# A silu gate whose 1/(1+exp(-z)) is made on ScalarE as exp(-ln(1+exp(-z))), with VectorE clamping the input

## What is computed

```
y_att = o_att * jax.nn.silu(ag.astype(f32))
y_hg  = o_hg * jax.nn.silu(hg.astype(f32))
ret_out  = rms_norm(ro).reshape(B, S, RET_W) * jax.nn.silu(rg)
diff_out = (...) * jax.nn.silu(dg)
lru_out  = rg_lru(...) * jax.nn.silu(lg)
```

## Time and profile before

| | |
|---|---|
| median of 3 runs | 3411.26 us (3410.83 to 3414.91) |
| the profiled execution's own time | 3415.89 us |
| its span, first to last instruction | 3414.0 us |
| TensorE matmul busy | 3176.8 us, 93% |
| VectorE busy | 1807.2 us, 53% |
| ScalarE busy | 1129.8 us, 33% |
| GpSimd busy | 1307.2 us, 38% |
| mean granted TensorE clock | 0.968 |

### The profile page before, as it was taken

How to read it: one execution, slowest core, us unless ns; L and a number is a source line. 1 busy time by engine, 2 the same in 40 slices (tenths; PEclk the granted TensorE clock), 3 DMA queues, 4 the chain that set the end, 5 groups by cost and what they waited for, 6 DMA issues and landing times.

```text
span 3414.0 us, 43651 instructions
## 1 busy us (share of the span) xinstructions
PE 3176.8 (93%) x14102; PEld 2497.3 (73%) x14102; DVE 1807.2 (53%) x2314; ACT 1129.8 (33%) x2000; POOL 1307.2 (38%) x1005
## 2 busy tenths in 40 slices
PE   8999999999999997988999999989779999999895
PEld 6877777777777785866877777768667777777684
DVE  5867667544544315557365764451273756555413
ACT  5333333233333433333232223333332332333332
POOL 4433333333333343433433433334334434333344
PEclk9999999999999998988999999999899999999998
DMA  5322121122121421223322222132233222222322
GB/s 217 111 86 74 61 74 62 62 74 72 63 74 69 165 90 60 96 88 109 132 74 84 79 74 80 66 124 98 77 120 121 77 81 90 74 74 74 123 93 92
DMA packets 60424, 308.54 MB, mean 90 GB/s; under 512 B 5536, under 2 KB 5920, under 8 KB 28832
## 3 DMA queue, kind: packets, MB, share of 16 engines
q1 hardware_dynamic: 34992, 254.82, 21.0%
q10 hardware_dynamic: 25328, 52.37, 4.3%
HBM read 288.81 MB, written 18.35 MB: 90 GB/s over the span
## 4 chain that ended last, share of the span: by engine, by line
PE 65%; DVE 21%; DVEq 5%; issue 5%; ACT 2%; POOL 1%; ACTq 0%; DMA 0%; POOLq 0%
PE z L252 54%; DVE work L916 5%; PE scores L291 2%; DVE work L1046 2%; PE scores L375 1%; DVEq L1120 1%; PE o_bank L344 1%; DVE work L1035 1%; POOL w_low L215 1%; DVE work L910 1%; DVE work L974 1%; DVEq L1201 1%; DVE work L1182 1%; PE scores L325 1%; PE o_bank L310 1%
## 5 line engine op out<-in xcount | busy, mean ns | idle before, releaser
L215 POOL TENSOR_TENSOR w_low<-w_raw,w_high 128x512 fp32r<-128x512 f32 x968 | 1289.6, 1338 | 2077.9 <-ACT w_high L508 2067.2
L252 PE MATMUL z<-u_high,w_high 128*128 128x512 f32 x3744 | 1537.9, 411 | 87.8 <-DVE u_low L1167 38.3
L252 PE MATMUL z<-u_low,w_high 128*128 128x512 f32 x3744 | 1476.5, 394 | 0.0
L252 PE MATMUL z<-u_high,w_low 128*128 128x512 f32 x3744 | 1476.5, 394 | 0.0
L508 ACT ACTIVATE w_high<-w_raw 128x512 fp32r<-128x512 f32 x968 | 601.6, 628 | 1492.6 <-PE z L252 1454.5
L252 PEld LDWEIGHTS z<-u_high,w_high 128*128 128x128 f32 x3744 | 713.1, 190 | 300.4 <-issue 62.6
L252 PEld LDWEIGHTS z<-u_low,w_high 128*128 128x128 f32 x3744 | 714.2, 191 | 153.8 <-issue 13.4
L252 PEld LDWEIGHTS z<-u_high,w_low 128*128 128x128 f32 x3744 | 712.8, 190 | 154.8
L1182 DVE TENSOR_TENSOR work<-work 128x512 f32<-128x512 f32 x90 | 104.4, 1161 | 441.0 <-ACT work L688 427.1
L916 DVE RECIPROCAL work<-work 128x512 f32<-128x512 f32 x88 | 295.1, 3353 | 6.5
L910 DVE TENSOR_TENSOR work<-z,work 128x512 f32<-128x512 f32 x114 | 78.9, 692 | 182.8 <-PE z L252 173.0
(11 more groups left out here) (189 smaller groups left out, 2327.0 us busy)
## 6 DMA issues: line engine op xcount, KB each, us to landing
w_raw<-in_wt SPq DMA_DIRECT2D x243, 1024.0 KB, 4.7
out_hT<-work ACTq DMA_DIRECT2D x10, 1024.0 KB, 9.8
work<-in_xT ACTq DMA_DIRECT2D x8, 1024.0 KB, 12.5
work<-out_hT ACTq DMA_DIRECT2D x8, 1024.0 KB, 13.1
e_scratch<-work ACTq DMA_DIRECT2D x1, 4096.0 KB, 16.6
work<-e_scratch ACTq DMA_DIRECT2D x1, 4096.0 KB, 22.4
work<-in_gw ACTq DMA_DIRECT2D x2, 1792.0 KB, 11.8
work<-in_dec ACTq DMA_DIRECT2D x12, 256.0 KB, 2.6
```

The lines of the kernel that those rows point to most:

```text
L215: pool.tensor_tensor(WL[:, 4 * q:4 * q + 4, :], RAW[:, t.odd, 512 * q:512 * q + 512].rearrange("p (k c) -> p k c", k=4), WH[:, 4 * q:4 * q ...
L252: mm = pe.matmul(bank[:], w[:, k, :], u[:, k, :], start=(k == 0 and n == 0), stop=(k == KT - 1 and n == 2))
```

## The change

ScalarE's `gate_exp` at the 48 gates becomes `gate_sigmoid`: it waits for a new signal `g_bounded`, and makes exp(-x), ln(x + 1) and exp(-x) in place on TM, with a drain between each two. VectorE's new `bounded` writes TM = max(RW, -42) right behind `rstd_mul`, and signals. VectorE's `sigmoid_of` (add 1, reciprocal) goes from the gates. ScalarE no longer waits for `z_free` there. The other users of `sigmoid_of` and of `gate_exp` (the recurrence steps) stay as they were.

```diff
+GATE_MIN = -42.0
...
+            def gate_sigmoid(n):
+
+                act.wait_ge(sem("g_bounded"), n + 1)
+                act.activation(row(TM), row(TM), ACT.Exp, scale=-1.0)
+                act.drain()
+                act.activation(row(TM), row(TM), ACT.Ln, bias=ONES[:, 0:1])
+                act.drain()
+                act.activation(row(TM), row(TM), ACT.Exp, scale=-1.0).then_inc(sem("gexp"), 1)
+
...
-                    if (gate and p == 15) or (gates and q == 3):
-                        gate_exp(t.plus(s))
+                    if gate is not None and p == 15:
+                        gate_sigmoid(gate)
+                    if gates is not None and q == 3:
+                        gate_sigmoid(gates + s)
...
             def gate_exps(*tiles):
                 for m in tiles:
-                    gate_exp(Tile(T_HGG + m))
+                    gate_sigmoid(m)
...
                     for q in range(4):
                         high(t, q)
-                    gate_exp(t)
+                    gate_sigmoid(l * 16 + 26 + m)
...
+            def bounded():
+
+                v.drain()
+                v.tensor_scalar(row(TM), row(RW), GATE_MIN, None, ALU.max).then_inc(sem("g_bounded"), 1)
+
             def gate_tile(t, n, dst, bank=None):

                 rstd_mul(t, row(RW), bank)
+                bounded()
                 v.wait_ge(sem("gexp"), n + 1)
-                sigmoid_of(TM)
                 v.tensor_tensor(dst, row(RW), row(TM), ALU.mult)
                 v.drain()

...
                 rstd_mul(Tile(T_L2 + R_LG + 5, (PER_LAYER, l)), row(RW))
+                bounded()
                 low(l * 32 + 64, MIX[:], b=8)
                 v.drain()
                 v.wait_ge(sem("gexp"), gl + 16)
-                sigmoid_of(TM)
                 v.tensor_tensor(row(RW), row(RW), row(TM), ALU.mult)
```

More of the change, by code:

```diff
@@ L637, in _, with step @@
             WORK = {"hg": hg_work, "att": att_work, "ret": ret_work, "dif": dif_work}
-            def step(t, gate=False, gates=False, hg=False, work=None, j=None, between={}, **kw):
+            def step(t, gate=None, gates=None, hg=False, work=None, j=None, between={}, **kw):
                 for p in range(16):
@@ L785, in _ @@
                 step(Tile(T_HG, (4, i)), hg=True, work="hg", j=i - 1)
-            step(Tile(T_ATT), gate=True, work="hg", j=HG_HEADS - 1)
+            step(Tile(T_ATT), gate=8, work="hg", j=HG_HEADS - 1)
             act.wait_ge(sem("hg_done"), PRIMED + HG_HEADS)
             with act.Fori(1, PAIRS) as i:
-                step(Tile(T_ATT, (4, i)), gate=True, work="att", j=i - 1)
+                step(Tile(T_ATT, (4, i)), gate=i + 8, work="att", j=i - 1)
             def finished_tile(p):
@@ L866, in _ @@
                 act.dma_start(W[:, GW:GW + 7, :], gw[l].rearrange("p (r t) -> p r t", r=7)).then_inc(sem("gw_loaded"), 16)
[L867 removed]
+                step(Tile(T_L2 + R_RET, (PER_LAYER, l)), gate=l * 16 + 16)
                 for h in range(1, RET_HEADS + 1):
[L869 removed]
+                    step(Tile(T_L2 + R_RET + 4 * h, (PER_LAYER, l)), gate=l * 16 + (16 + h), work="ret", j=l * RET_HEADS + h - 1,
                          load=h if h < RET_HEADS else None, b=h - 1, cl=l + 1 if h == 1 else None)
@@ L873, in _ @@
                 with act.Fori(1, DIF_HEADS) as i:
-                    step(Tile(T_L2 + R_DIF, (PER_LAYER, l), (4, i)), gate=True, work="dif",
+                    step(Tile(T_L2 + R_DIF, (PER_LAYER, l), (4, i)), gate=l * 16 + i + 22, work="dif",
                          j=l * DIF_HEADS + i - 1)
-                step(Tile(T_L2 + R_LG, (PER_LAYER, l)), gates=True, work="dif", j=l * DIF_HEADS + DIF_HEADS - 1)
+                step(Tile(T_L2 + R_LG, (PER_LAYER, l)), gates=l * 16 + 26, work="dif", j=l * DIF_HEADS + DIF_HEADS - 1)
                 for m in range(4, LRU_TILES):
```

2 lines of the change are left out of this document (removed).

## The result

| | before | after |
|---|---|---|
| median of 4 runs each | 3412.01 us (3410.83 to 3414.91) | 3369.70 us (3366.53 to 3373.27) |
| the profiled execution's own time, its span | 3415.89, 3414.0 us | 3372.59, 3370.7 us |
| TensorE matmul busy | 3176.8 us, 93% | 3167.0 us, 94% |
| VectorE, ScalarE busy | 1807.2, 1129.8 us | 1650.3, 1191.4 us |
| mean granted TensorE clock | 0.968 | 0.971 |

The ratio is 0.9873, with a 95% interval of 0.986 to 0.9887: 42 us faster, 43.3 between the two profiles. The forecast was 3362 us, a gain of 49.

A forecast was written before the change was run, and what follows sets the result against it. TensorE, nearly full, was taken to bound the kernel, so only its idle time behind gates counts: waits 38.4 us plus clock 11.2 make 49.6, say 49, giving 3362 us; range 3345 to 3389.

The forecast's parts named there:

- The gate's own price: Each changed gate, norm product to gate product: 2.7 us instead of 4.76, so 2.0 us shorter on VectorE.
- a maximum that runs at half pace: Pessimistic bound on one gate: slower maximum and 0.3 us more per drain make it 3.7 us, saving only 1.0.
- First gates and attention: Ahead of the layers: TensorE's wait at 108.05 goes, 1.4 us; 2.0 us of attention's single 6.6 us wait comes back.
- Retention: Retention steps: TensorE's ten 0.5 us waits for the decay product go, 5.2 us in all.
- Differential: Differential steps, each layer: 2.0 of the 4.42 us softmax wait, and 1.7, 1.6 and 1.1 whole; 1.2 us of clock.
- LRU gates: Step with LRU gates, each layer: softmax waits give back 1.7, 2.0 and 2.0 us, plus clock where waits shrink.
- The clock's 3.3: LRU step: full TensorE clock expected once the 2.46 and 3.01 us waits fall to 0.5 and 1.0; 1.7 + 1.6 us.
- End of a layer: TensorE's first u_low wait grows from 2.84 to 4.8 us, the second shrinks; gain 2.8 us in waits, 3.9 with clock.
- The net 1.1 of the clock: Layer's end: clock time regained, allowing that the longer first wait may itself lower the clock; 1.1 us a layer.
- The rival of a late ScalarE: In-order ScalarE delays splits and softmax exponential; threshold about 2 us in retention, near 0 in differential steps; 3437 us, chance 0.06.
- TensorE as the bound: Whole kernel: each removed wait meets another, so under 7 us gained, about 3407 us; chance of hidden gain 0.06.
- the clock stays: Waits shrink but no granted clock returns: 38 us less, 3373 us; chance 0.20 for waits without clock.

The follow-up runs named there:

- e1: Changed kernel without the maximum (lower bound) at the gates, ScalarE reading the normed value itself: 3350.5 us, ratio 0.9816 to before.
- e2: Changed kernel with ScalarE's sigmoid ahead of that quarter's split in the LRU step, bound kept: 3359.9 us, ratio 0.9848 to before.
- e7: Changed kernel with the maximum made twice in a row at every silu gate: 3388.6 us, ratio 0.9922 to before.
- e5: Changed kernel run again with nothing edited: 3364.9 us, ratio 0.9852 to before.
- e3: Changed kernel with only each layer's last gate back in the old form (exponential, then VectorE addition and reciprocal): 3371.4 us, ratio 0.9880 to before.
- e4: Changed kernel with each layer's last sigmoid moved behind ScalarE's first eight u_high tiles: 3359.3 us, ratio 0.9847 to before.
- e10: Changed kernel with four small extra copies on ScalarE behind each silu gate's sigmoid: 3398.4 us, ratio 0.9958 to before.
- e8: Changed kernel with eight small extra copies on ScalarE behind each silu gate's sigmoid: 3453.2 us, ratio 1.0113 to before.

## Why the prediction was right, and where its steps were off

The forecast was 3362 us and the medians are 3369.7 and 3364.9. The mechanism was right: shorter gates give back TensorE's waits in the layers, and some of its clock. That the total came out close owes something to errors of both signs: in the first layer the retention and differential steps gave 3.4 us more than forecast, the LRU step and the end 4.7 less. The terms:

- **The gate's own price**: 2.7 forecast, 2.85 measured in a differential step. Right there. In the LRU step the gate takes 3.78 (end of L922 at 2171.92 to L941 at 2175.70), because the maximum takes 1.49. I had this case only as a bound ("a maximum that runs at half pace"), and took 0.43 everywhere from one row of another place. That is the term that was mis-sized: e1 gets 4.7 us a layer back in the LRU step, e2 2.1, e7 loses 4.0.
- **First gates and attention**: forecast 1.4 and 2.0. The wait of 1.39 went, and the 6.64 became 4.73. But the profile had only 0.9 us to show at 1728, and the stretch ahead of the layers varies by more than that between executions (e5). Both profiles that I compared have the long wait at 185 us, so that at least doesn't stand between them.
- **Retention**: forecast 2.6 a layer; five steps, from 1728.18 to 2002.99 before and from 1727.29 to 1997.87 after, gained 4.2. The ten waits went. The row showed 0.50 us of idle time, but it cost more than that: from the pair of score matmuls ahead of the wait to the pair behind it it is 4.07 us before (1791.33 to 1795.40) and 3.41 after (1789.30 to 1792.71), and the pair behind takes 0.70 instead of 0.59. That makes 0.8 us, all that a step in the middle of the stage gained (54.2 to 53.4).
- **Differential**: the 1.7, 1.6 and 1.1 went whole, the 4.42 became 2.11. I wrote that no row shows a low clock behind a wait under 2 us and "I take there to be none". One did, behind the 1.62 us wait of before: 0.67 over 2129.30 to 2134.00. It was not among my rows, and it is 1.6 of the 2.0 us by which that stretch gained more than forecast. It is no rule either: in the second layer of before the clock is 1.00 behind the like wait (1.61 us at 3063.98). At the first wait I had 1.2 us for the clock, half of 2.3, and 0.8 came (2.5 us lost before, 1.7 after); in the first layer of e5, behind the same wait, all of it.
- **LRU gates**: 10.1 forecast, 7.3 measured. The clock's 3.3 came in the first layer, since the clock was full although waits of 1.5 and 1.8 stayed. The waits fell short by 2.7, through the maximum and the product beside GpSimd. In the second layer there was less clock to give back, and the step gained 5.9: I had taken the first layer's stretches for both, but of the kernel before the clock was full there behind the 2.46.

```profile
3145.20:3150.00 4.80, 4.74 (x25) 3.58 (x25) 0.71 (x3) 1.75 (x3) 1.85 (x2) 1.00 0.00 0
```

- **End of a layer**: 3.9 forecast, 2.0 measured against before, 2.8 against e3, where only this gate differs. The first wait is 5.39 instead of 4.8, and the second 0.57, as forecast: 2.4 from the two where I had 2.8. The net 1.1 of the clock is the term that didn't come: its mean over the end is 0.92 before and after, 0.89 in e3. The longer wait isn't shown to be the cause of the fall behind it, since e3 and e4 have 0.64 and 0.69 behind 2.84 and 2.95 us.
- **The rival of a late ScalarE** was rightly refused for this change, and rightly priced as a danger. Its threshold in the retention steps (2.0 us) lies where e10 and e8 put it (1.6 to 3.1). In the differential ones I had it near 0; e10 shows only that a delay of 1.9 us is over it. Its price was too low: for 3 us more I had 3437, e8 has 3453, because each late softmax also meets GpSimd and then costs the clock.
- **Two readings of rows** were off without touching the sum: the chain holds 26 reciprocals of 3.35 us in the layers, not 25, and the table load stands not only around the sines but once at 9 us too, seven in all, the same seven after the change.
- **TensorE as the bound** (3407) and **the clock stays** (3373): the first is refused. The second isn't far from the slower executions, but its mechanism, no clock given back, is refused by the LRU stretches at 1.00.

## What to carry to other kernels

Moving a function from the engine on the path to one beside it is worth what the busy engine idles behind it, and it costs wherever that other engine's program order stands on the path: the same edit gained 42 us at the gates and lost 11 at the recurrence, there in part to its own helper operation. Price such an operation at the place where it will run, from its slowest row as well as its usual one: a maximum of 0.43 us cost up to 1.56 where the order of the program put it beside a split of GpSimd, and leaving it out, which needs an argument that the input stays in range, was worth 16 us by the medians, 11.5 of them traced. Before comparing profiles of one execution each, look at a stretch that the change can't touch, and before counting on a fall of the clock, look at whether the next layer repeats it.

## What the runs showed of the hardware

- A collision of VectorE with GpSimd is seen only as a longer instruction: the same 128x512 maximum has a shortest time of 426 ns and a longest of 1564, and an operation on 128x128 elements takes 0.28 or 1.37 us. No wait is booked.

```profile
L934 DVE TENSOR_SCALAR work<-work x48: 426/428/1564, 78.1 to 3150.9; 128x512 f32<-128x512 f32 x48
```

- All 18 lengthened maxima end 0.28 or 0.29 us after the split in which they began; 13 that began in its last 0.13 us kept their 0.43.
- One program took either 3363.9 to 3366.8 or 3372.6 to 3373.3 us. Profiles with the same code differ from some 180 us on by one such collision and the clock behind it (3.5 us), and by a second stretch of low clock from 630 us.
- The clock did not follow the length of the last wait: 1.00 behind 1.77 us (2196.77 after) and 0.67 behind 1.62 (2129.39 before), and at one and the same place 0.64 or 1.00 behind 2.11 us (two executions of one program) and 1.00 or 0.64 behind 2.84 (before and e3).
